# Where a convolution's filter spectra are computed: in three row norms, or tile by tile beside their use

## The chip, the cores and the metric

The kernel runs on one core of a Trainium2 chip. A core has a matrix engine (TensorE, PE in the profile), a vector engine (VectorE, DVE), a scalar engine (ScalarE, ACT), GpSimd (POOL) and the queue of SyncE (SP), which issues the transfers. They run side by side and wait for each other through semaphores. The metric is the device time of one execution in microseconds (us). Three executions of the kernel before took 2008.16, 2002.99 and 2000.46 us, median 2002.99 us.

## The reference, cut to what matters

256 tokens of width 1024 go through two transformer layers (attention and a gated feed-forward part each), then through a block that mixes a gated recurrence (HGRN) with a long convolution (Hyena), and through a large expert layer. What the change touches is the convolution's filter, one per channel:

```python
    h_f, h_b = hyena_filters(L, filt_w1, filt_b1, filt_freq1, filt_w2, filt_b2, filt_freq2,
                             filt_w3, filt_decay)
    y_b = x0 * bidirectional_fftconv(v * x1, h_f, h_b, hyena_bias)
...
    uf = jnp.fft.rfft(uf32, n=2 * L, axis=1)
    kf = jnp.fft.rfft(kern, n=2 * L, axis=0)
    y = jnp.fft.irfft(uf * kf[None], n=2 * L, axis=1)[:, :L]
```

`kern` is put together from the forward and the backward taps, which come from weights alone. So `kf`, the filter's spectrum, does not depend on the tokens and can be computed at any time before the product. The kernel computes both spectra by multiplying with a table of cosines and sines (`dft`, for a transform of length 511): the real part of the filter's from the sum of the two taps (`filt_sum`), the imaginary part from their difference (`filt_dif`).

## The kernel before, in words

Everything is held with channels on the 128 partitions and the 256 tokens beside each other, so a matrix of width 1024 is eight column tiles. Weights come in slabs of 128 x 1024 through a ring of three buffers. ScalarE copies each slab to a rounded "lead" (L260), VectorE subtracts to get the "rest" (L266), and TensorE multiplies both parts (L282, L401, L414). The order of the work on each engine is written out by hand; no scheduler moves anything.

**The row norms.** There are four stages "p0" to "p3", one after each half of the two layers. In each, ScalarE squares a half of the rows (L642), takes the root (L645), VectorE the reciprocal (L697), both scale it (L648, L699), and TensorE turns it back with eight transposes (L684), once for each half of the tokens. Then VectorE adds to the residual `xT` (L704), ScalarE and VectorE make the parts `hsplit` for the next stage (L726, L736), and TensorE begins with it (L401, 12 matmuls for each quarter of the channels). After p0, p1 and p2 there is also a late norm (L749, 32 records of one column) after the third quarter.

**The spectra.** `spectrum_tensor` (L658) computes the spectrum of one channel tile with four matmuls of 256 columns in full float32 (L664), each of which is two records in the profile. The tiles are spread as `SPECTRA_AT` says: none in p0, three in p1, three in p2, two in p3, the first behind the first eight transposes and the others behind the second eight. ScalarE copies them later to `filt_sum` and `filt_dif` (L671), over the taps that they were made from, so nothing else is held. `spectra_read_tensor` makes TensorE wait for the copies before it uses the banks again.

**Clearing the feed-forward output.** Each feed-forward stage clears four PSUM banks with four matmuls of zeros (L462). In layer 0 that stands behind the row norm p0. In layer 1 the spectra lie in these banks, so it stands after the fourth quarter.

**The Hyena stage.** It runs once for each of the eight channel tiles n. On TensorE (`hyena_tile_tensor`): transposes of the input u (L2193), one slab of weights for the next tile (24 matmuls, "filler", L282), the spectrum of u (L2198), two more fillers, transposes of the product (L2206), a fourth filler, and the inverse transform (L2211). On VectorE (`hyena_tile_vector`): the rest of a slab, a part of the HGRN norm (L2158 to L2160), the two spectral products (L2298), the sum and difference (L2303, L2304), rests of slabs and the short convolution that makes the next u. On ScalarE: the copies of the PSUM results and the leads. At n = 0 there is also one root over 2048 columns (L2153) of the sums in banks 4 to 7.

Of the kernel before, what the change touches and what calls it, by code (L numbers as in the profile page):

```python
# [30 lines left out]
P = 128  # L31
D = 1024
# [94 lines left out]
def build(nc, weights, small, tables, masks, w3, decay, subkeys, gain_row, x, out):  # L127
# [309 lines left out]
    def ffn_tensor(pe, layer, pre):  # L437
# [35 lines left out]
        if layer == 1:  # L473
            clear()
# [25 lines left out]
    def ffn_scalar(act, layer, pre):  # L500
# [27 lines left out]
        if layer == 1:  # L528
            spectra_scalar(act, "p2")
# [122 lines left out]
    SPECTRA_AT = {"p0": (), "p1": (0, 1, 2), "p2": (3, 4, 5), "p3": (6, 7)}  # L652

    def spectrum(n):

        return strided(filt_sum, n * P, [[2 * D, 2], [D, 2], [1, P]])

    def spectrum_tensor(pe, st, k):  # L658
        n = SPECTRA_AT[st][k]
        if n == 0:  # L660
            pe.wait_ge(S("filters", "taps"), FILTER_BLOCKS - 2)
        for part, taps in enumerate((filt_sum, filt_dif)):
            for a in range(2):
                mm = pe.matmul(ps[:, 1 + k, part * T:(part + 1) * T], taps[:, a, n * P:(n + 1) * P],  # L664
                               dft[:, a, part * T:(part + 1) * T], start=(a == 0), stop=(a == 1))
        mm.then_inc(S("hyena", "spectra"), 1)

    def spectra_scalar(act, st):
        for k, n in enumerate(SPECTRA_AT[st]):
            act.wait_ge(S("hyena", "spectra"), n + 1)  # L670
            act.activation(spectrum(n), ps[:, 1 + k, :].rearrange("p (b a c) -> p b a c", b=2, a=2),  # L671
                           ACT.Copy).then_inc(S("hyena", "spectra_sb"), 1)

    def spectra_read_tensor(pe, st):
        pe.wait_ge(S("hyena", "spectra_sb"), SPECTRA_AT[st][-1] + 1)

    def rows_norm_tensor(pe, st):
        for tt in range(TT):
            for c in range(KC):
                if c == 0:  # L680
                    pe.wait_ge(S("rows", "scalar"), rows_at(st, 6, 3 * tt + 3))
                if c == 4:
                    pe.wait_ge(S("rows", "vector"), rows_at(st, 4, 2 * tt + 2))
                mm = pe.transpose(YB[:, c, tt * P:(tt + 1) * P], y_rows[:, tt, c * P:(c + 1) * P], eye)  # L684
                if tt == TT - 1 and c % 2:
                    mm.then_inc(S("rows", "tensor"), 1)
            for n in range(len(SPECTRA_AT[st])):
                if min(n, 1) == tt:
                    spectrum_tensor(pe, st, n)
# [112 lines left out]
    dft = table("dft").rearrange("p (a f) -> p a f", a=2)  # L802
# [182 lines left out]
    def fox_scalar(act, st):  # L985
# [32 lines left out]
        act.wait_ge(S("hgrn", "bounds"), 1)  # L1018
        act.activation(lbe, lbd, ACT.Exp).then_inc(S("hgrn", "bounds"), 1)
# [109 lines left out]
    def moba_tensor(pe, st):  # L1129
        pe.wait_ge(S("norm", "x"), x_steps("p1") + 2)  # L1130
        for g, bank in enumerate((4, 2)):
            if g == 1:
                spectra_read_tensor(pe, "p1")
            for q in range(4):
# [3 lines left out]
                if g == 1 and q == 1:  # L1138
# [3 lines left out]
                    mm.then_inc(S(st, "factor"), 1)  # L1142
# [58 lines left out]
    def moba_scalar(act, st):  # L1201
# [12 lines left out]
        spectra_scalar(act, "p1")  # L1214
# [35 lines left out]
    def moba_vector(v, own, st):  # L1250
# [33 lines left out]
        v.wait_ge(S(st, "factor"), 2)  # L1284
# [622 lines left out]
    def hgrn_tensor(pe, st):  # L1907
# [8 lines left out]
        for j in range(5):  # L1916
            if j == 2:
                spectra_read_tensor(pe, "p3")
# [89 lines left out]
    def hgrn_scalar(act, st):  # L2008
# [13 lines left out]
        spectra_scalar(act, "p3")  # L2022
# [77 lines left out]
    def bounds_logits_vector(v, own, st):  # L2100
        l2 = small_("lbl").rearrange("p (a h) -> p a h", a=2)
        own(v.tensor_tensor(lbs, l2[:, 0, :], l2[:, 1, :], ALU.max))
        v.tensor_tensor(lbd, l2, lbs.unsqueeze(1).to_broadcast([P, 2, HH]), ALU.subtract).then_inc(S(st, "bounds"), 1)

    def bounds_vector(v, own, st):
        v.wait_ge(S(st, "bounds"), 2)
# [62 lines left out]
    uT = carve(TT, P)  # L2169
    prod_a, prod_b = carve(2, T), carve(2, T)  # L2170
    yspec = carve(4, P)
    yspecT = carve(4, P)
    conv_y = carve(T)
    idft = table("idft").rearrange("p (a f) -> p a f", a=4)
# [15 lines left out]
    def hyena_tile_tensor(pe, st, n):  # L2190
# [39 lines left out]
    def hyena_tile_scalar(act, st, n):  # L2230
# [5 lines left out]
        lead_scalar(act, *filler(4 * n + 2))  # L2236
        lead_scalar(act, *filler(4 * n + 3))
# [49 lines left out]
    def hyena_tile_vector(v, own, st, n):  # L2287
# [4 lines left out]
        if n == 0:  # L2292
            v.wait_ge(S(st, "spectra_sb"), KC)
        v.wait_ge(S(st, "uspec"), n + 1)

        def times(dst, part):
            half = ps[:, 3, part * T:(part + 1) * T].rearrange("p (a c) -> p a c", a=2)
            return v.tensor_tensor(dst[:, :, :].rearrange("p b (a c) -> p b a c", a=2),  # L2298
                                   half.unsqueeze(1).to_broadcast([P, 2, 2, P]), spectrum(n), ALU.mult)
        times(prod_a, 0)  # L2300
        own(times(prod_b, 1))
        f = yspec[:, :, :].rearrange("p a c -> p (a c)")
        v.tensor_tensor(f[:, 0:T], prod_a[:, 0, :], prod_b[:, 1, :], ALU.subtract)  # L2303
        v.tensor_tensor(f[:, T:2 * T], prod_a[:, 1, :], prod_b[:, 0, :], ALU.add).then_inc(S(st, "yspec"), 1)  # L2304
# [251 lines left out]
    def early_tensor(pe, st, stream):  # L2556
        pe.wait_ge(S("final", "x_rows"), 2)
# [31 lines left out]
    def picks_vector(v, own, st):  # L2589
# [15 lines left out]
        v.wait_ge(S("final", "x_rows"), 2)  # L2605
# [181 lines left out]
    def x_rows_tensor(pe, pre):  # L2787
# [4 lines left out]
        mm.then_inc(S("final", "x_rows"), 1)  # L2792

    def x_rows_scalar(act):
        act.wait_ge(S("final", "x_rows"), 1)
# [384 lines left out]
```

## Time and profile before

| | |
|---|---|
| Three executions | 2008.16, 2002.99, 2000.46 us |
| The profiled execution | 2008.16 us, of which the traced span is 2006.1 us |
| TensorE busy (matmul records) | 1954.2 us, 97% |
| TensorE weight loads busy | 1728.1 us, 86% |
| VectorE busy | 1340.2 us, 67% |
| ScalarE busy | 1008.5 us, 50% |
| Mean granted TensorE clock | 0.983 of full |

The profiled execution is the slowest of the three. TensorE's matmul records overlap, so its share is an upper view of its work. PEclk in a row is the share of the full clock that was granted in that stretch: 1.00 is 2.4 GHz and 0.50 is 1.2 GHz.

### The profile page before, as it was taken

To read this page: it belongs to the slowest core of one execution; us is meant where nothing else is said; L and a number is where in the kernel's file an instruction comes from. 1 tells how busy PE (TensorE), PEld (TensorE's weight loads), DVE (VectorE), ACT (ScalarE), POOL (GpSimd) and SP (SyncE) were. 2 spreads that over 40 slices of the span, in tenths; PEclk is the share of its full clock that TensorE was granted. 3 is DMA by queue.
4 is the path that set the end of the run, shared out by engine and by line. 5 is a ranking of instruction groups with operands and counts; after the bars stand their busy time and mean duration, and the time that the engine had idled before them with its cause. 6 is when DMAs were issued, how large, how long until landed. Compare 5 with 4: busy or idle time off the path is not lost.

```text
span 2006.1 us, 34432 instructions
## 1 busy us (share of the span) xinstructions
PE 1954.2 (97%) x12338; PEld 1728.1 (86%) x12338; DVE 1340.2 (67%) x2732; ACT 1008.5 (50%) x1632; POOL 320.4 (16%) x138
## 2 busy tenths in 40 slices
PE   7998999999999999999999999999999999999998
PEld 6775788778788888999899989999999998888886
DVE  6356556656655557889898689933667766666666
ACT  5336546555554446666544455665444443433333
POOL 0000000000000000000000057877666600000000
PEclk9799899999999999999999999999999999999999
DMA  6142465544335554444344535555444455555554
GB/s 230 62 150 73 147 209 180 162 132 137 102 130 189 188 188 137 148 144 131 105 143 143 178 126 169 181 174 168 138 140 145 137 162 195 190 197 188 195 191 157
DMA packets 85150, 313.99 MB, mean 157 GB/s; under 512 B 9456, under 2 KB 9456, under 8 KB 84592
## 3 DMA queue, kind: packets, MB, share of 16 engines
q1 hardware_dynamic: 85040, 312.49, 47.2%
q8 instruction: 73, 1.20, 0.3%
q14 instruction: 37, 0.30, 0.1%
HBM read 311.40 MB, written 1.05 MB: 156 GB/s over the span
## 4 chain that ended last, share of the span: by engine, by line
issue 61%; PE 32%; POOL 6%; DVE 0%; POOLq 0%; DVEq 0%; ACT 0%
PE ps L414 17%; PE ps L282 12%; POOL wsplit L266 6%; PE ps L2683 3%; PE ps L430 0%; DVE work L2813 0%; DVE sq L2720 0%; POOLq L265 0%; PE ps L2759 0%; POOLq L2546 0%; DVE sq L2716 0%; DVE picks L2636 0%; PE ps L2649 0%; DVEq L2971 0%; DVE work L2728 0%
## 5 line engine op out<-in xcount | busy, mean ns | idle before, releaser
L260 ACT ACTIVATE wsplit<-ring 128x1024 fp32r<-128x1024 f32 x572 | 603.8, 1057 | 506.4 <-PE ps L414 268.9
L266 DVE TENSOR_TENSOR wsplit<-ring,wsplit 128x1024 fp32r<-128x1024 f32 x438 | 535.0, 1224 | 330.0 <-ACT wsplit L260 328.5
L282 PE MATMUL ps<-hsplit,wsplit 128*128 128x256 f32 x5064 | 652.3, 288 | 7.1 <-DVE hsplit L736 2.1
L282 PEld LDWEIGHTS ps<-hsplit,wsplit 128*128 128x128 f32 x5064 | 625.3, 194 | 18.0 <-issue 9.1
L266 POOL TENSOR_TENSOR wsplit<-ring,wsplit 128x1024 fp32r<-128x1024 f32 x134 | 320.2, 2396 | 1291.3 <-ACT wsplit L260 1291.3
L414 PE MATMUL ps<-wsplit,gsplit 128*128 128x512 f32 x1992 | 456.5, 390 | 0.0
L414 PEld LDWEIGHTS ps<-wsplit,gsplit 128*128 128x128 f32 x1992 | 373.2, 188 | 81.5 <-issue 4.2
L401 PE MATMUL ps<-wsplit,hsplit 128*128 128x512 f32 x1248 | 305.7, 402 | 12.6 <-DVE wsplit L266 10.7
L401 PEld LDWEIGHTS ps<-wsplit,hsplit 128*128 128x128 f32 x1248 | 238.2, 193 | 64.9 <-issue 13.8
L1825 PE MATMUL ps<-hsplit,wsplit 128*128 128x256 f32 x936 | 128.5, 288 | 0.0
L1825 PEld LDWEIGHTS ps<-hsplit,wsplit 128*128 128x128 f32 x936 | 116.3, 191 | 0.0
L2720 DVE TENSOR_SCALAR sq<-ps,picks 128x128 f32<-128x128 f32 x256 | 87.0, 404 | 0.0
L2740 DVE TENSOR_TENSOR work<-ps,work 128x216 f32<-128x216 f32 (+31 forms) x64 | 32.9, 514 | 74.0 <-ACT work L2708 74.0
L2382 PE MATMUL ps<-hsplit,wsplit 128*128 128x256 f32 x576 | 71.4, 285 | 0.7 <-DVE hsplit L2363 0.4
L2382 PEld LDWEIGHTS ps<-hsplit,wsplit 128*128 128x128 f32 x576 | 69.7, 192 | 2.1 <-DVE wsplit L266 0.8
L2683 PE MATMUL ps<-sq 128*128 128x128 f32 x512 | 67.6, 275 | 0.3 <-DVE sq L2720 0.3
L2696 ACT ACTIVATE work<-ps 128x252 f32<-128x252 f32 (+62 forms) x63 | 17.5, 278 | 99.7 <-PE ps L282 99.7
L2683 PEld LDWEIGHTS ps<-sq 128*128 128x128 f32 x512 | 62.6, 192 | 0.5 <-DVE sq L2720 0.5
L1936 ACT ACTIVATE work<-work 128x256 f32<-128x256 f32 x128 | 48.7, 430 | 23.8 <-DVE work L2078 17.8
L304 DVE TENSOR_TENSOR gsplit<-work,gsplit 128x256 fp32r<-128x256 f32 x128 | 54.4, 425 | 4.4
L2567 ACT ACTIVATE work<-ps 128x256 f32 x54 | 20.8, 385 | 58.2 <-PE ps L282 58.1
L1894 PE MATMUL ps<-work 128*128 128x128 f32 x288 | 43.9, 275 | 0.7 <-ACT work L1936 0.7
(316 smaller groups left out, 1697.7 us busy)
## 6 DMA issues: line engine op xcount, KB each, us to landing
ring<-in_weights SPq DMA_DIRECT2D x580, 512.0 KB, 3.3
work<-in_tables SPq DMA_DIRECT2D x1, 2123.0 KB, 12.6
xT<-in_x SPq DMA_DIRECT2D x1, 1024.0 KB, 5.1
work<-in_subkeys SPq DMA_DIRECT2D x1, 1024.0 KB, 15.2
work<-in_decay SPq DMA_DIRECT2D x2, 512.0 KB, 4.1
out_x<-work SPq DMA_DIRECT2D x2, 512.0 KB, 2.6
work<-in_w SPq DMA_DIRECT2D x1, 512.0 KB, 6.6
ring<-in_gain_row SPq DMA_DIRECT2D x1, 512.0 KB, 3.7
```

What stands on the lines that cost most here:

```text
L260: act.activation(wsplit[:, n % RING, 0, :], slab(s), ACT.Copy).then_inc(S("split", "lead"), 1)
L266: eng.tensor_tensor(wsplit[:, n % RING, 1, :], slab(s), wsplit[:, n % RING, 0, :], ALU.subtract).then_inc(S("split", RESTS[stream][0]), 1)
L282: mm = pe.matmul(dst, wsplit[:, n, a, c * P:(c + 1) * P], hsplit[:, b, c, :], start=(c == 0 and t == 0), stop=(c == KC - 1 and t == 2))
L304: v.tensor_tensor(gsplit[:, slot, 1, :], src, gsplit[:, slot, 0, :], ALU.subtract).then_inc(sem, 1)
L401: mm = pe.matmul(ps[:, bank + tt, :], hsplit[:, b, c, tt * P:(tt + 1) * P], wsplit[:, n, a, cc * 512:(cc + 1) * 512], start=(c == 0 and t ...
L414: mm = pe.matmul(YR[:, tt, half * 512:(half + 1) * 512], gsplit[:, slot, b, tt * P:(tt + 1) * P], wsplit[:, n, a, half * 512:(half + 1) * ...
L1825: mm = pe.matmul(dst, wsplit[:, n, a, c * P:(c + 1) * P], hsplit[:, b, c, :], start=(c == 0 and t == 0), stop=(c == KC - 1 and t == 2))
L1894: mm = pe.matmul(dst[:, a, :], k_[:, a * P:(a + 1) * P], q_[:, b * P:(b + 1) * P], start=True, stop=True)
L1936: ins = act.activation(strided(mixed, (l % 2 * 2 + x_) * T, [[2 * size, n], [size, 2], [1, size]]), strided(qakb, x_ * 2 * T, [[2 * size, ...
L2382: mm = pe.matmul(branch(m), wsplit[:, n, a, c * P:(c + 1) * P], hsplit[:, b, c, :], start=(c == 0 and t == 0), stop=(c == KC - 1 and t == 2))
L2683: mm = pe.matmul(ps[:, 6 + b % 2, k * P:(k + 1) * P], hots[:, b % 2, 1, k, :], hots[:, b % 2, 0, k, :], start=True, stop=True)
L2720: ins = v.tensor_scalar(hots[:, b % 2, 0, k, :], ps_iota, picks[:, 0, t:t + 1], picks[:, 2, t:t + 1], ALU.is_equal, ALU.mult)
```

## The change

The spectra are no longer computed in the row norms. Each is computed in the Hyena stage, in its own tile, between the spectrum of u and the second filler, in PSUM bank 4. ScalarE copies it to a new buffer `kspec` with two activations (512 columns, and 256 columns of the cosine part again), and the VectorE product waits for these. The products are the same in number and shape, only their operands are laid out otherwise. The clear of layer 1 stands where that of layer 0 stands. At n = 0 the wait for the root of the HGRN norm moves ahead of the new matmuls, since that root reads bank 4. Some semaphores are split into two names, which changes no order.

```diff
-        def clear():
-            if layer == 1:
-                spectra_read_tensor(pe, "p2")
-            for y in range(4):
-                pe.matmul(ps[:, y, :], zeros[:, :], zero_rows(), start=True, stop=False, skip_group_check=True)
-
-        if layer == 0:
-            clear()
+        for y in range(4):
+            pe.matmul(ps[:, y, :], zeros[:, :], zero_rows(), start=True, stop=False, skip_group_check=True)
         pe.wait_ge(S("norm", "x"), x_steps(POST[pre]) + 2)
...
         pe.wait_ge(S("late", "scalar"), LATE_NORMS.index(pre) * 5 + 5)
-        if layer == 1:
-            clear()
...
-    SPECTRA_AT = {"p0": (), "p1": (0, 1, 2), "p2": (3, 4, 5), "p3": (6, 7)}
...
-            for n in range(len(SPECTRA_AT[st])):
-                if min(n, 1) == tt:
-                    spectrum_tensor(pe, st, n)
...
     # hyena_tile_tensor
         for a in range(TT):
-            mm = pe.matmul(ps[:, 3, :], uT[:, a, :], dft[:, a, :], start=(a == 0), stop=(a == 1))
-        mm.then_inc(S(st, "uspec"), 1)
+            pe.matmul(ps[:, 3, :], uT[:, a, :], dft[:, a, :], start=(a == 0), stop=(a == 1))
+        if n == 0:
+            pe.wait_ge(S("hnorm", "root"), 1)
+        for part, taps in enumerate((filt_sum, filt_dif)):
+            for a in range(2):
+                mm = pe.matmul(ps[:, 4, part * T:(part + 1) * T], taps[:, a, n * P:(n + 1) * P], dft[:, a, part * T:(part + 1) * T],
+                               start=(a == 0), stop=(a == 1))
+        mm.then_inc(S(st, "spectra"), 1)
         filler_tensor(pe, st, n, 1)
         filler_tensor(pe, st, n, 2)
-        if n == 0:
-            pe.wait_ge(S("hnorm", "root"), 1)
         pe.wait_ge(S(st, "yspec"), n + 1)
...
     # hyena_tile_scalar
         lead_scalar(act, *filler(4 * n + 2))
+        act.wait_ge(S(st, "spectra"), n + 1)
+        act.activation(kspec[:, 0:2, :].rearrange("p a t -> p (a t)"), ps[:, 4, :], ACT.Copy).then_inc(S(st, "kspec"), 1)
+        act.activation(kspec[:, 2, :], ps[:, 4, 0:T], ACT.Copy).then_inc(S(st, "kspec"), 1)
         lead_scalar(act, *filler(4 * n + 3))
...
     # hyena_tile_vector
-        if n == 0:
-            v.wait_ge(S(st, "spectra_sb"), KC)
-        v.wait_ge(S(st, "uspec"), n + 1)
...
+        v.wait_ge(S(st, "kspec"), 2 * n + 1)
+        uspec = ps[:, 3, :].rearrange("p (a t) -> p a t", a=2)
+        v.tensor_tensor(prod_a[:, :, :], uspec, kspec[:, 0:2, :], ALU.mult)
+        v.wait_ge(S(st, "kspec"), 2 * n + 2)
+        own(v.tensor_tensor(prod_b[:, :, :], uspec, kspec[:, 1:3, :], ALU.mult))
```

On TensorE, in the feed-forward stage of layer 1, this stood in a row before, from the end of the attention output (L788) over the row norm p2 to the first quarter inside the loop:

```order
L788 MATMUL ps<-wsplit,hsplit 128x512 x24
L684 MATMUL ps<-eyeiota,work 128x128 x8
L664 MATMUL ps<-work 128x256 x4
L684 MATMUL ps<-eyeiota,work 128x128 x8
L664 MATMUL ps<-work 128x256 x8
L401 MATMUL ps<-wsplit,hsplit 128x512 x36
L749 MATMUL ps<-ones,sq 128x1 x16
L401 MATMUL ps<-wsplit,hsplit 128x512 x12
L462 MATMUL ps<-zeros 128x512 x4
```

The same place in the changed kernel (its lines 750, 649, 459 and 711 are 788, 684, 462 and 749 before):

```order
L750 MATMUL ps<-wsplit,hsplit 128x512 x24
L649 MATMUL ps<-eyeiota,work 128x128 x16
L459 MATMUL ps<-zeros 128x512 x4
L401 MATMUL ps<-wsplit,hsplit 128x512 x36
L711 MATMUL ps<-ones,sq 128x1 x16
L401 MATMUL ps<-wsplit,hsplit 128x512 x12
```

Twelve float32 matmuls are gone between and behind the transposes, and the four clears have moved ahead of the quarters. In p1 and p3 the spectra go too (12 and 8 matmuls), and nothing takes their place.

One tile of the Hyena stage on TensorE before, from the transposes of u to the inverse transform:

```order
L2193 MATMUL ps<-eyeiota,work 128x128 x2
L282 MATMUL ps<-hsplit,wsplit 128x256 x24
L2198 MATMUL ps<-work 128x512 x2
L282 MATMUL ps<-hsplit,wsplit 128x256 x48
L2206 MATMUL ps<-eyeiota,work 128x128 x4
L282 MATMUL ps<-hsplit,wsplit 128x256 x24
L2211 MATMUL ps<-work 128x256 x4
```

The same tile in the changed kernel, where L2160 is the spectrum of the filter:

```order
L2150 MATMUL ps<-eyeiota,work 128x128 x2
L282 MATMUL ps<-hsplit,wsplit 128x256 x24
L2155 MATMUL ps<-work 128x512 x2
L2160 MATMUL ps<-work 128x256 x4
L282 MATMUL ps<-hsplit,wsplit 128x256 x48
L2167 MATMUL ps<-eyeiota,work 128x128 x4
L282 MATMUL ps<-hsplit,wsplit 128x256 x24
L2172 MATMUL ps<-work 128x256 x4
```

Four matmuls of 256 columns are added to each of eight tiles; the rest stands as it stood.

## Rows read from the trace of the kernel before

**Rows 1.** The page's busy times: engine, us, share of the span, instructions.
```profile
PE 1954.2 (97%) x12338; PEld 1728.1 (86%) x12338; DVE 1340.2 (67%) x2732; ACT 1008.5 (50%) x1632; POOL 320.4 (16%) x138
```

**Rows 2.** Timeline, Hyena tile 0: start, us, engine, line, operation, count, idle before.
```profile
970.81 1.97 ACT L2153 ACTIVATE work<-ps,eps_tile 128x2048 f32<-128x2048 f32 x1
...
973.10 6.30 PE L282 MATMUL ps<-hsplit,wsplit 128*128 128x256 f32 x48
...
977.85 1.28 DVE L2298 TENSOR_TENSOR work<-ps,work 128x512 f32<-128x512 f32 x2
...
980.08 0.63 PE L2206 MATMUL ps<-eyeiota,work 128*128 128x128 f32 x4 [0.67 <-DVE work L2304]
981.12 3.13 PE L282 MATMUL ps<-hsplit,wsplit 128*128 128x256 f32 x24 [0.41 <-DVE wsplit L266]
...
987.20 3.13 PE L282 MATMUL ps<-hsplit,wsplit 128*128 128x256 f32 x24 [1.01 <-DVE wsplit L266]
```

**Rows 3.** Windows, one later Hyena tile: PE, PEld, DVE, ACT, POOL busy, clock, DMA.
```profile
1018.60:1034.20 15.60, 15.60 (x117) 14.39 (x116) 14.94 (x25) 6.25 (x9) 0.00 (x0) 1.00 0.40 136
```

**Rows 4.** Timeline of that tile, the steps that the new matmuls touch.
```profile
1021.33 1.88 PE L2198 MATMUL ps<-work 128*128 128x512 f32 x4
...
1024.13 1.28 DVE L2298 TENSOR_TENSOR work<-ps,work 128x512 f32<-128x512 f32 x2
...
1032.10 1.89 PE L2211 MATMUL ps<-work 128*128 128x256 f32 x8
1032.20 2.36 DVE L266 TENSOR_TENSOR wsplit<-ring,wsplit 128x1024 fp32r<-128x1024 f32 x2
...
1033.83 0.38 PE L2193 MATMUL ps<-eyeiota,work 128*128 128x128 f32 x2
```

**Rows 5.** Line 671, the copy of a spectrum: count, ns min/median/max, first and last start.
```profile
L671 ACT ACTIVATE work<-ps x8: 575/584/600, 439.7 to 786.9; 128x512 f32<-128x512 f32 x8
```

**Rows 6.** Timeline of TensorE, row norm p0 and the start behind it (no spectra).
```profile
216.94 1.09 PE L684 MATMUL ps<-eyeiota,work 128*128 128x128 f32 x8 [1.58 <-ACT work L648]
...
220.30 10.99 PE L401 MATMUL ps<-wsplit,hsplit 128*128 128x512 f32 x36 [1.30 <-DVE hsplit L736]
231.13 3.63 PE L749 MATMUL ps<-ones,sq 128*128 128x1 f32 x32
...
241.80 0.60 PE L446 MATMUL ps<-eyeiota,sq 128*128 128x128 f32 x4
```

**Rows 7.** The same for row norm p1 (three spectra).
```profile
427.18 1.09 PE L684 MATMUL ps<-eyeiota,work 128*128 128x128 f32 x8
428.11 3.62 PE L664 MATMUL ps<-work 128*128 128x256 f32 x16
431.38 8.74 PE L401 MATMUL ps<-wsplit,hsplit 128*128 128x512 f32 x36
439.95 3.62 PE L749 MATMUL ps<-ones,sq 128*128 128x1 f32 x32
```

**Rows 8.** The same for row norm p2 (three spectra, clear in the later place).
```profile
567.30 1.09 PE L684 MATMUL ps<-eyeiota,work 128*128 128x128 f32 x8
...
588.06 1.03 PE L462 MATMUL ps<-zeros 1*128 1x512 bf16 x4
589.03 3.06 PE L401 MATMUL ps<-wsplit,hsplit 128*128 128x512 f32 x12
591.92 0.60 PE L446 MATMUL ps<-eyeiota,sq 128*128 128x128 f32 x4
```

**Rows 9.** The same for row norm p3 (two spectra, norm of the HGRN input).
```profile
765.88 1.09 PE L684 MATMUL ps<-eyeiota,work 128*128 128x128 f32 x8
...
769.24 2.99 PE L401 MATMUL ps<-wsplit,hsplit 128*128 128x512 f32 x12 [0.54 <-DVE hsplit L736]
772.07 3.61 PE L365 MATMUL ps<-sq,ones 128*128 128x256 f32 x16
```

**Rows 10.** Windows behind p0, p1 and p3, columns as in rows 3.
```profile
218.00:220.00 2.00, 1.00 (x5) 0.26 (x4) 1.81 (x5) 1.67 (x4) 0.00 (x0) 0.73 0.00 0
224.00:226.00 2.00, 2.00 (x7) 1.57 (x6) 1.75 (x5) 2.00 (x5) 0.00 (x0) 0.57 0.09 35
...
430.00:432.00 2.00, 2.00 (x10) 1.74 (x10) 2.00 (x4) 0.27 (x1) 0.00 (x0) 1.00 0.00 0
...
769.00:770.00 1.00, 0.76 (x3) 0.67 (x4) 1.00 (x2) 1.00 (x3) 0.00 (x0) 1.00 0.00 0
```

More of the change, by code:

```diff
@@ L650, in rows_norm_scalar @@
             lead_scalar(act, leads, 1)
-    SPECTRA_AT = {"p0": (), "p1": (0, 1, 2), "p2": (3, 4, 5), "p3": (6, 7)}
[L654 to L659, printed above, removed]
-        if n == 0:
[L661 to L675, printed above, removed]
     def rows_norm_tensor(pe, st):
@@ L801, in build @@
     SEGS = ((1, 0, T), (0, T, P))
-    dft = table("dft").rearrange("p (a f) -> p a f", a=2)
     pos[0] = era
@@ L1017, in fox_scalar @@
         act.preload_act_table(ACT.Exp)
-        act.wait_ge(S("hgrn", "bounds"), 1)
-        act.activation(lbe, lbd, ACT.Exp).then_inc(S("hgrn", "bounds"), 1)
+        act.wait_ge(S("hgrn", "lbd"), 1)
+        act.activation(lbe, lbd, ACT.Exp).then_inc(S("hgrn", "lbe"), 1)
         lead_scalar(act, st, 6)
@@ L1283, in moba_vector @@
         moba_rest(v, 6)
-        v.wait_ge(S(st, "factor"), 2)
+        v.wait_ge(S(st, "factors"), 1)
         by_token = ps[:, 7, 0:T].unsqueeze(1).to_broadcast([P, 2, T])
@@ L2102, in bounds_logits_vector @@
         own(v.tensor_tensor(lbs, l2[:, 0, :], l2[:, 1, :], ALU.max))
-        v.tensor_tensor(lbd, l2, lbs.unsqueeze(1).to_broadcast([P, 2, HH]), ALU.subtract).then_inc(S(st, "bounds"), 1)
+        v.tensor_tensor(lbd, l2, lbs.unsqueeze(1).to_broadcast([P, 2, HH]), ALU.subtract).then_inc(S(st, "lbd"), 1)
     def bounds_vector(v, own, st):
-        v.wait_ge(S(st, "bounds"), 2)
+        v.wait_ge(S(st, "lbe"), 1)
         own(v.tensor_tensor(lbs, lbe[:, 0, :], lbe[:, 1, :], ALU.add))
@@ L2169, in build @@
     uT = carve(TT, P)
+    kspec = carve(3, T)
     prod_a, prod_b = carve(2, T), carve(2, T)
@@ L2173, in build @@
     conv_y = carve(T)
+    dft = table("dft").rearrange("p (a f) -> p a f", a=2)
     idft = table("idft").rearrange("p (a f) -> p a f", a=4)
@@ L2291, in hyena_tile_vector @@
             hgrn_norm_vector(v, own, "hnorm", n)
-        if n == 0:
-            v.wait_ge(S(st, "spectra_sb"), KC)
-        v.wait_ge(S(st, "uspec"), n + 1)
[L2296 to L2301, printed above, removed]
+        v.wait_ge(S(st, "kspec"), 2 * n + 1)
[3 more added lines that the diff above has]
+        own(v.tensor_tensor(prod_b[:, :, :], uspec, kspec[:, 1:3, :], ALU.mult))
         f = yspec[:, :, :].rearrange("p a c -> p (a c)")
-        v.tensor_tensor(f[:, 0:T], prod_a[:, 0, :], prod_b[:, 1, :], ALU.subtract)
-        v.tensor_tensor(f[:, T:2 * T], prod_a[:, 1, :], prod_b[:, 0, :], ALU.add).then_inc(S(st, "yspec"), 1)
+        v.tensor_tensor(f[:, 0:T], prod_a[:, 0, :], prod_a[:, 1, :], ALU.subtract)
+        v.tensor_tensor(f[:, T:2 * T], prod_b[:, 0, :], prod_b[:, 1, :], ALU.add).then_inc(S(st, "yspec"), 1)
         rest_of(v, *filler(4 * n + 3))
@@ L2556, in early_tensor @@
     def early_tensor(pe, st, stream):
-        pe.wait_ge(S("final", "x_rows"), 2)
+        pe.wait_ge(S("final", "x_rows"), 1)
         with pe.Fori(0, EARLY // 6) as i:
@@ L2603, in picks_vector @@
             own(v.tensor_scalar(best[:, tt, 0:6, :], best[:, tt, 0:6, :], row_stats[:, 2, tt:tt + 1], None, ALU.mult))
-        v.wait_ge(S("final", "x_rows"), 2)
+        v.wait_ge(S("final", "x_rows"), 1)
         v.tensor_copy(ps_iota, iota)
@@ L2791, in x_rows_tensor @@
                 mm = pe.transpose(YR[:, tt, c * P:(c + 1) * P], xT[:, c, tt * P:(tt + 1) * P], eye)
-        mm.then_inc(S("final", "x_rows"), 1)
+        mm.then_inc(S("final", "x_turned"), 1)
     def x_rows_scalar(act):
-        act.wait_ge(S("final", "x_rows"), 1)
+        act.wait_ge(S("final", "x_turned"), 1)
         act.activation(x_rows[:, :, :], YR, ACT.Copy).then_inc(S("final", "x_rows"), 1)
```

10 lines of the change are left out of this document (1 added, 9 removed).

## The prediction

> **What bounds the kernel now.** I read the page first. TensorE's matmul records fill 97% of the span [rows 1], but they overlap, so this alone does not say that a microsecond more of matmul is a microsecond more of time. That has to be read at the two places of the change: where the spectra leave, and where they go.
>
> Where they go is the Hyena stage. The windows of one tile [rows 3] show TensorE busy for all of 15.60 us, VectorE 14.94 and ScalarE 6.25, with the clock at 1.00. The timeline of TensorE repeats with 15.58 us from tile to tile and has no idle entry from tile 1 to tile 6, and one of a few tenths at most at tile 7. So in tiles 1 to 7 TensorE is the bound, with VectorE close behind. Tile 0 is different [rows 2]: there TensorE waits 0.67 us for VectorE's product (L2304), 0.41 us for a slab's rest and 1.01 us for the next one (L266). VectorE sets that tile.
>
> Where they leave is the row norms. p0 has no spectra and the feed-forward stage behind it is built like the one behind p2. So p0 is a model, in this very trace, of what p2 becomes, and nearly one for p1. [Rows 6] show that TensorE idles 1.58 us ahead of the second transposes and 1.30 us ahead of the first quarter, and [rows 10] that the granted clock is 0.73 over 218 to 220 us and 0.57 over 224 to 226 us, and 0.50 between: it is at its lower level, 1.2 GHz, from about 218.9 to 225.7 us. Ahead of that fall TensorE had done nothing but transposes, waits and the four clears since 214.3 us. Behind p1 and p3 the clock reads 1.00 [rows 10]; there the spectra stood between and behind the transposes.
>
> **The Hyena stage.** The added work is four float32 matmuls of 256 columns for each tile, two records each. The trace has the same form in the inverse transform L2211: 8 records from 1032.10 us, and the next operation starts at 1033.83 [rows 4], so 1.73 us. The two spectra in a row in p1 agree: 16 records in 3.62 us, the tail of the last included [rows 7]. In tiles 1 to 7 there is no idle time to hide this: 7 x 1.73 = 12.1 us.
>
> In tile 0 the new matmuls would begin where the second filler begins, at 973.10 us. The root that they now wait for ends at 970.81 + 1.97 = 972.78 [rows 2], so that wait costs nothing, by 0.3 us. The 1.73 us push the product's transposes from 980.08 to about 981.1, since the 0.67 us of waiting goes. Then the slab's rest comes on time (0.41 goes), and the third wait, 1.01 us for a rest that VectorE delivers at 987.2 by its own chain, takes up what is left of 1.73 - 0.67 - 0.41 = 0.65 us. So tile 0 costs 0, if VectorE is not delayed there. If it is by the whole amount, 1.7 us; I keep that end for the range.
>
> Is VectorE delayed? The changed product waits for ScalarE's copy of the spectrum. In a tile the product starts 2.80 us after the spectrum of u begins (1021.33 to 1024.13 [rows 4]). After the change the matmuls end at about 1.3 + 1.73 = 3.05 us, the first copy takes 0.58 us [rows 5] with some 0.3 us of waking, so the product starts at about 3.95, 1.1 us later. The second copy has half the columns, so at most 0.58 us, and ends while the first product (0.64 us) runs. VectorE's 14.94 us and this 1.1 us are 16.0, under the new tile of 15.6 + 1.7 = 17.3. Queued behind the waiting product are the sum and difference, the slab's rest, the short convolution and the next u. What TensorE needs of these latest is the next slab's rest: VectorE starts it at 1032.20, has it at about 1033.4, and TensorE wants it at about 1034.0 [rows 4]. It moves by 1.1 us and TensorE by 1.7, so the slack grows. In tile 0 VectorE reaches its product only at 977.85 us [rows 2], long after the copies (about 976.0), so nothing is added. ScalarE has 6.25 of 15.6 us busy [rows 3]; 1.2 us more, between two leads, fits. Its lead for the fourth filler comes some 2 us later, still ahead of VectorE's rest of it.
>
> The Trainium skill would price these matmuls otherwise. "TensorE: Matmul & The Clock Gate", section "Back-to-back issue gap", lists 262 cycles for 256 columns, 0.11 us at full clock. By that table an added tile would be 4 x 0.11 = 0.44 us and seven of them 3.1 us, and the whole change about +7 us. The row on the same form shows two records a matmul and 1.73 us for four, so the trace does not agree with that figure for float32 operands, and the measurement decides.
>
> The Trainium skill's front page, "Trainium Kernel Development and Optimization", section "Best Practices", also says to judge TensorE by the share of weight loads and not by matmul busy time. That share is 14.39 of 15.60 us in a tile [rows 3], which read so would leave 1.2 us per tile for the new work and make the seven tiles 7 x 0.5 = 3.7 us. I do not take it, because the added work is itself a stream of load and matmul pairs behind a stream of the same.
>
> **The row norms.** p2: from the second transposes to the first transposes of the loop (L446) it is 591.92 - 567.30 = 24.62 us before [rows 8], and 241.80 - 216.94 = 24.86 us in p0 [rows 6]. That is the changed order exactly, clears included, so +0.24 us. It is made of two parts that nearly cancel: the quarters start earlier and the clears leave the busy stretch (588.06 to 589.03, 1.0 us), but the three quarters run partly at 1.2 GHz (10.99 against 8.74 us, [rows 6, 7]).
>
> p1: from the second transposes to the late norm it is 439.95 - 427.18 = 12.77 us [rows 7], and 231.13 - 216.94 = 14.19 us in p0 [rows 6]: +1.42 us. There the quarters would begin 3.36 us after the transposes in place of 4.20 (a gain of 0.84), and lose 2.25 to the clock. p1 has no clear to move.
>
> p3: TensorE started its first quarter 3.36 us after the transposes already [rows 9], as in p0, and it waited 0.54 us, so nothing is gained. The loss is that of p0, 2.25 us, if the clock falls. Part lies on the first 12 matmuls (2.99 us at full clock) and the rest on the sums L365 behind them, and the root, the reciprocal and the whole norm of the HGRN input hang on these sums. So I take +2.2 us, all on the path. Bounds for p1 and p3: with no fall -0.84 and 0; with all of the first stretch at the lower level the 8.74 us of [rows 7] would double, so +7.9 and, by the 6.6 us of [rows 9], +6.6. The nearest row is p0, and I use it.
>
> ScalarE's eight copies (0.58 us each) leave these stages; no wait of TensorE hangs on them, so 0.
>
> **The sum.** 12.1 + 0 + 0.24 + 1.42 + 2.2 = 16.0 us. The profiled execution took 2008.16 us with a span of 2006.1, so its counterpart would have a span of 2022.1 and take 2024.2. The median of before lies 5.2 us under the profiled one, so as a median I forecast 2003.0 + 16.0 = 2019.0 us.
>
> **The rivals.**
>
> *The clock does not fall.* Transposes and short gaps do not bring it down in p1, p2 and p3. For it: in p3 before, TensorE idled about half a microsecond at 1.00. Against it: p0. Then the norms give -0.84, -0.84 - 1.0 and 0, together -2.7, and the change is +9.4: 2012.4 us, at the edge of 0.5%. If only one of p1 and p3 keeps its clock, it is about 2.2 less than forecast, 2016.8.
>
> *VectorE becomes the bound of the Hyena tiles.* The product waits for ScalarE, and something behind it, the next u or a rest, comes too late for TensorE. For it: 14.94 of 15.60 us busy [rows 3]. Against it: the slack worked out above. If each of seven tiles lost the whole 1.1 us again: +7.7, so 2026.7 us.
>
> *VectorE is the bound of these tiles already.* This is the one that ends without a loss that can be told. If TensorE's full busy time in tiles 1 to 7 hid slack, as its 2.1 us in tile 0 did, the matmuls would vanish in it and only the norms would be left: 2003.0 + 3.9 = 2006.9 us. It decides so only if VectorE's own chain needs 17.3 us for a tile; its busy time is 14.94, and TensorE has no wait entry there, which is why it is small.
>
> **How the numbers follow.** Forecast 0.78; the clock does not fall (anywhere) 0.08; VectorE late behind the copies 0.07; VectorE the bound already 0.04; the rest 0.03, of which 0.01 for a kernel that gains. 0.5% is 10 us, about what a measurement of this kernel can tell from no change, so the line is at 2013.0. Slower by over 0.5%: 0.78 + 0.07 + about a quarter of 0.08 + 0.01 = 0.88. Within: 0.11. Faster: 0.01. The range: the low end is the case without a fall of the clock, 2012.4; the high end takes 1.7 for tile 0 and some 3 us more of low clock, 2024, and 2 us more for the scatter of medians in executions that spread over 7.7 us. So 2012 to 2026.
>
> **What would show it.** Hyena tiles 1 to 6 at 17.3 us each in place of 15.58, TensorE without idle entries. Tile 0 as long as before, its 0.67 and 0.41 us gone and about 0.35 us of the third wait left. A product that starts about 1.1 us later in its tile. The clock near 0.5 for some 5 us behind p1, p2 and p3. From p1's second transposes to its late norm 14.2 us, and 24.9 us for p2's stretch. The forecast is wrong if the tiles grow by clearly less than 1.7 us, or if the clock behind p1 and p3 reads 1.00.

## The result, and the profile after

The changed kernel took 2016.21 us in the median of four executions (2012.11 to 2020.97), the kernel before 2001.72 us (four, 1998.60 to 2008.16). The ratio is 1.0076, 95% interval 1.0057 to 1.0094: 15 us slower, 11 to 19. The forecast was a loss of 16.0 us.

The two traces by themselves say less: the span is 2011.9 us against 2006.1, 5.8 us more. The difference from the 14.5 us between the medians lies in work that the change does not touch, and this is the first thing to read. The second transposes of p0 stand at 216.94 us before [rows 6] and at 210.08 after, with nothing changed ahead of them but the lines' numbers and two semaphores' names. Here are two windows of that part in the trace of the kernel before (columns as in [rows 3]):

```profile
50.00:60.00 10.00, 9.25 (x52) 8.59 (x52) 4.59 (x15) 4.41 (x12) 0.00 (x0) 0.75 0.15 53
90.00:100.00 10.00, 9.10 (x43) 7.68 (x43) 3.52 (x14) 3.92 (x11) 0.00 (x0) 0.53 0.11 35
```

And the same two windows in the trace of the changed kernel:

```profile
50.00:60.00 10.00, 9.25 (x57) 7.11 (x57) 3.82 (x8) 3.41 (x12) 0.00 (x0) 1.00 0.34 109
90.00:100.00 10.00, 10.00 (x81) 10.00 (x81) 4.91 (x9) 6.04 (x8) 0.00 (x0) 0.94 0.32 107
```

The granted clock reads 0.75 and 0.53 in the one and 1.00 and 0.94 in the other: it fell at other moments of the same sequence. So I compare the traces stage by stage, between operations that both have, and not by their ends. From the start to the second transposes of p0 the changed kernel's trace is 6.9 us shorter, from there to p1's 1.0 and on to p2's 2.1 us shorter. From p2's to p3's it is equal to 0.1 us. Then it is 1.6 us longer up to the Hyena stage, 11.9 us longer in it and 2.3 us longer behind it: 5.8 us in all. Of the last 2.3 us, 1.6 are one more spell at the lower clock (0.50 from 1654.5 to 1657.9 us), which the traces of two experiments on the kernel before have as well.

**Hyena.** TensorE's timeline of tiles 0 and 1 in the changed kernel (start, us, engine, line, operation, count, idle before):

```profile
960.30 0.38 PE L2150 MATMUL ps<-eyeiota,work 128*128 128x128 f32 x2
...
965.11 1.89 PE L2160 MATMUL ps<-work 128*128 128x256 f32 x8
966.65 6.10 PE L282 MATMUL ps<-hsplit,wsplit 128*128 128x256 f32 x48
972.59 0.60 PE L2167 MATMUL ps<-eyeiota,work 128*128 128x128 f32 x4
972.94 3.12 PE L282 MATMUL ps<-hsplit,wsplit 128*128 128x256 f32 x24
...
978.79 3.14 PE L282 MATMUL ps<-hsplit,wsplit 128*128 128x256 f32 x24 [0.79 <-DVE wsplit L266]
```

In tile 0 the waits of 0.67 and 0.41 us [rows 2] are gone and the third has shrunk from 1.01 to 0.79 us. From the first transposes to the next tile's first filler it is 978.79 - 960.30 = 18.49 us; before, 987.20 [rows 2] - 968.69 = 18.51, counted from this row of the kernel before:

```profile
968.69 0.38 PE L2193 MATMUL ps<-eyeiota,work 128*128 128x128 f32 x2
```

The waits were worth more than their entries say. The product's transposes start 12.29 us behind the first ones where it was 11.39, so 0.90 of the 1.73 us came through and the wait of 0.67 had been worth 0.83. The filler behind them starts 0.35 us later where it was 1.04, so the wait of 0.41 had been worth 0.69. An idle entry counts from the end of the last record, and without a wait the next operation starts before that end (the four transposes' row lasts 0.60 us, and the filler starts 0.35 us into it). The later tiles follow each other in 17.31 us where it was 15.58. One window of 17.30 us, which answers to [rows 3]:

```profile
1030.00:1047.30 17.30, 17.30 (x124) 15.88 (x123) 14.97 (x25) 7.01 (x11) 0.00 (x0) 1.00 0.38 122
```

TensorE is busy for all of it, VectorE for 14.97 us (14.94 before). The steps of tile 1, which answer to [rows 4]:

```profile
999.08 1.88 PE L2155 MATMUL ps<-work 128*128 128x512 f32 x4
...
1000.80 1.89 PE L2160 MATMUL ps<-work 128*128 128x256 f32 x8
...
1002.72 0.60 ACT L2199 ACTIVATE work<-ps 128x512 f32<-128x512 f32 x1 [4.98 <-PE ps L2160]
1003.22 0.38 ACT L2200 ACTIVATE work<-ps 128x256 f32<-128x256 f32 x1
...
1003.35 0.69 DVE L2258 TENSOR_TENSOR work<-ps,work 128x512 f32<-128x512 f32 x1 [1.40 <-ACT work L2199]
```

The product starts 4.27 us behind the spectrum of u (it was 2.80), 1.47 us later and not 1.1. The spectrum's records begin 1.72 us behind those of u, where I had 1.3, and the filler behind them starts at 1002.34, so the stream is through after 3.26 us and not 3.05. From there to the copy are 0.38 us, where I had 0.3.

**The row norms.** TensorE behind the second transposes of p1, p2 and p3, answering to [rows 7 to 9]:

```profile
419.31 1.09 PE L649 MATMUL ps<-eyeiota,work 128*128 128x128 f32 x8 [1.58 <-ACT work L638]
422.67 9.80 PE L401 MATMUL ps<-wsplit,hsplit 128*128 128x512 f32 x36 [2.26 <-DVE hsplit L698]
432.31 3.63 PE L711 MATMUL ps<-ones,sq 128*128 128x1 f32 x32
...
557.38 1.09 PE L649 MATMUL ps<-eyeiota,work 128*128 128x128 f32 x8 [1.57 <-ACT work L638]
560.74 10.71 PE L401 MATMUL ps<-wsplit,hsplit 128*128 128x512 f32 x36 [0.77 <-DVE hsplit L698]
...
581.95 0.60 PE L446 MATMUL ps<-eyeiota,sq 128*128 128x128 f32 x4
...
755.91 1.09 PE L649 MATMUL ps<-eyeiota,work 128*128 128x128 f32 x8 [1.58 <-ACT work L638]
759.27 4.58 PE L401 MATMUL ps<-wsplit,hsplit 128*128 128x512 f32 x12 [2.27 <-DVE hsplit L698]
763.68 3.62 PE L365 MATMUL ps<-sq,ones 128*128 128x256 f32 x16
```

Three windows of the same trace, behind the second transposes of p1, p2 and p3:

```profile
424.00:426.00 2.00, 2.00 (x7) 1.54 (x6) 2.00 (x7) 0.91 (x2) 0.00 (x0) 0.59 0.59 174
559.00:565.00 6.00, 5.23 (x13) 3.49 (x12) 5.68 (x13) 3.27 (x9) 0.00 (x0) 0.50 0.26 87
760.00:762.00 2.00, 2.00 (x6) 1.53 (x5) 2.00 (x6) 0.97 (x4) 0.00 (x0) 0.54 0.28 47
```

Each first quarter now has an idle entry ahead of it. The clock falls behind all three norms: it is at 0.50 for 3.4 us behind p1 and behind p3 (the windows of 2 us lie mostly in these spells) and for 6.8 us behind p2, where the prediction had some 5 us at each. p1's stretch is 13.00 us (12.77 before), p2's 24.57 (24.62), p3's to the sums 7.77 (6.19).

### The profile page after: what moved, and what is told of

Read it like the earlier page. It is cut to its first block, busy times and chain, and to the rows that moved or that the text cites. A ratio compares the mean times of both kernels' runs of the same rounds, so it can differ in the third digit from the quotient of the medians.

```text
span 2011.9 us, 34435 instructions
## 1 busy us (share of the span) xinstructions
PE 1953.4 (97%) x12338; PEld 1727.1 (86%) x12338; DVE 1340.9 (67%) x2732; ACT 1010.4 (50%) x1640; POOL 320.4 (16%) x138
## 4 chain that ended last, share of the span: by engine, by line
issue 61%; PE 32%; POOL 6%; DVE 0%; POOLq 0%; DVEq 0%; ACT 0%
PE ps L414 17%; PE ps L282 12%; POOL wsplit L266 6%; PE ps L2642 3%; PE ps L430 0%; DVE work L2772 0%; DVE sq L2679 0%; POOLq L265 0%; PE ps L2718 0%; POOLq L2505 0%; DVE sq L2675 0%; DVE picks L2595 0%; PE ps L2608 0%; DVEq L2930 0%; DVE work L2687 0%
## 5 line engine op out<-in xcount | busy, mean ns | idle before, releaser
L401 PE MATMUL ps<-wsplit,hsplit 128*128 128x512 f32 x1248 | 310.0, 406 | 17.2 <-DVE wsplit L266 10.6
```

Source lines behind the costliest of these rows:

```text
L401: mm = pe.matmul(ps[:, bank + tt, :], hsplit[:, b, c, tt * P:(tt + 1) * P], wsplit[:, n, a, cc * 512:(cc + 1) * 512], start=(c == 0 and t ...
```

## The experiments

All but one are timed against the kernel before, on the same chip. "Stretch" is always from the second transposes to the late norm (p1), to the first transposes of the loop (p2), or to the sums (p3).

**Norms alone.** The changed kernel with the Hyena stage's spectra taken out, shown shortened. It leaves out the filter's spectrum and its copies, and the product takes the taps in its place, so what it computes is not the block:

```diff
     # hyena_tile_tensor, hyena_tile_scalar
-        for part, taps in enumerate((filt_sum, filt_dif)):
-            for a in range(2):
-                mm = pe.matmul(ps[:, 4, ...], taps[:, a, n * P:(n + 1) * P], dft[...], ...)
-        act.activation(kspec[:, 0:2, :]..., ps[:, 4, :], ACT.Copy)
-        act.activation(kspec[:, 2, :], ps[:, 4, 0:T], ACT.Copy)
     # hyena_tile_vector
-        v.tensor_tensor(prod_a[:, :, :], uspec, kspec[:, 0:2, :], ALU.mult)
+        v.tensor_tensor(prod_a[:, :, :], uspec, filt_sum[:, :, 0:T], ALU.mult)
...
```

> The changed kernel's row norms (no spectra in p1, p2, p3, early clear) with no spectrum of the filter in the Hyena stage either: the four matmuls and both copies of each tile are left out, and the products take the taps in place of spectra. Theory A (the spectra kept TensorE's clock up behind the norms, and their going costs there): Hyena tiles 1 to 6 at 15.6 us as in the kernel before; behind p1, p2 and p3 the clock at 0.5 for some 3 to 5 us; in all +2.5 to +4 us against before, of which p3 +1.6, p1 +0.2 to +1.4, p2 about 0. Theory B (the clock's falls are not caused by the change and the norms gain from the matmuls and the clear that leave): -2.7 us against before. Theory C (all of the change's time is in the norms): +14 us.

Ratio 1.0003 (0.9991 to 1.0015), so 0.6 us more, between 1.8 less and 3.0 more. Hyena tiles 15.58 us. Theory C is out. Theory B's 2.7 us less lies outside the interval, but so does my own sum of 3.9 us for the norms, and most of theory A's 2.5 to 4. The stretches say why. The clock did fall behind p1: its stretch is 14.35 us, and the row of its first three quarters takes 11.15 us in TensorE's timeline of this kernel, against 8.74 at full clock in [rows 7]:

```profile
420.03 1.09 PE L649 MATMUL ps<-eyeiota,work 128*128 128x128 f32 x8 [1.58 <-ACT work L638]
423.38 11.15 PE L401 MATMUL ps<-wsplit,hsplit 128*128 128x512 f32 x36 [2.26 <-DVE hsplit L698]
...
437.86 8.45 PE L401 MATMUL ps<-wsplit,hsplit 128*128 128x512 f32 x36
```

But my stretch of p1 ends at the late norm, and behind it the time comes back. The last row above is the next three quarters, at full clock. In the kernel before they stand behind the late norm with a spell at 1.2 GHz in them:

```profile
443.44 10.07 PE L401 MATMUL ps<-wsplit,hsplit 128*128 128x512 f32 x36
```

Up to the end of these quarters (L1100, before L1141) p1 takes 26.13 us here and 26.17 before. p2's stretch is 23.94, 0.7 us shorter, and from p3 to the Hyena stage it is 204.38 us in place of 202.81. Together 0.9 us, which agrees with the 0.6 us timed. So the eight spectra, some 14 us of matmul, cost next to nothing where they stood.

**The matmuls twice.** The kernel before, with four more matmuls in each tile that nobody reads:

```diff
         mm.then_inc(S(st, "uspec"), 1)
+        if n == 0:
+            pe.wait_ge(S("hnorm", "root"), 1)
+            pe.wait_ge(S(st, "spectra_sb"), KC)
+        for part, taps in enumerate((filt_sum, filt_dif)):
+            for a in range(2):
+                pe.matmul(ps[:, 4, part * T:(part + 1) * T], taps[:, a, n * P:(n + 1) * P], dft[...], ...)
...
-        if n == 0:
-            pe.wait_ge(S("hnorm", "root"), 1)
```

> The kernel before, all spectra in the norms as they were, and in each Hyena tile the four matmuls again, into bank 4, read by nobody; no copies, no new wait of VectorE. Theory A (the price of the Hyena stage is TensorE's own time): tiles 1 to 6 at 17.3 us, tile 0 no longer than before, +12 us in all. Rival (the price comes from the product waiting for ScalarE's copies): tiles stay at 15.6 us and the time within 2 us of before.

Ratio 1.0062 (1.0047 to 1.0076), 9 to 15 us more. TensorE's timeline of this kernel over one tile, from its inverse transform (L2216) to the filler in the next one:

```profile
1014.87 1.89 PE L2216 MATMUL ps<-work 128*128 128x256 f32 x8
...
1019.68 1.88 PE L2198 MATMUL ps<-work 128*128 128x512 f32 x4
1021.39 1.89 PE L2205 MATMUL ps<-work 128*128 128x256 f32 x8
1022.93 6.09 PE L282 MATMUL ps<-hsplit,wsplit 128*128 128x256 f32 x48
```

Tiles 2 to 6 take 17.31 us, tiles 0 and 1 together 35.70 as in the changed kernel (35.69), with no copy and no new wait on VectorE. With the experiment above it splits the change: the Hyena matmuls are the loss. The two ratios give 12.4 and 0.6 us, and the changed kernel measured 12.8 us on the same chip (below).

**Warm norms.** The changed kernel with matmuls that nobody reads put back where the spectra were:

```diff
+    WARM_AT = {"p0": 0, "p1": 3, "p2": 3, "p3": 2}
     # rows_norm_tensor, behind each half's transposes
+            for n in range(WARM_AT[st]):
+                if min(n, 1) == tt:
+                    warm_tensor(pe, st, n)    # four matmuls of 256 columns, float32
```

> The changed kernel with 3, 3 and 2 times four float32 matmuls put back at the places where the spectra stood in p1, p2 and p3, into banks that nobody reads; the spectra that count stay in the Hyena stage, and the clear stays early. Theory A (clock): the clock stays at 1.00 behind p1, p2 and p3 until the late norm; p1's stretch from the second transposes to the late norm 12.8 us, p3's first twelve matmuls 3.0 us in place of 4.6, and the time 2 to 4 us less than the changed kernel's, though work is added. Theory B (the matmuls in the norms cost their time, the clock is not theirs): 1.7 us more than the changed kernel, 0.84 in each of p1 and p2.

TensorE's timeline of this kernel behind the second transposes of p1:

```profile
423.29 1.09 PE L659 MATMUL ps<-eyeiota,work 128*128 128x128 f32 x8
424.22 3.62 PE L649 MATMUL ps<-work 128*128 128x256 f32 x16
427.49 8.73 PE L401 MATMUL ps<-wsplit,hsplit 128*128 128x512 f32 x36
```

p1's stretch is 12.77 us, p3's 6.18, and from p3 to the Hyena stage 202.76 us. The clock stays up where these matmuls stand: theory A on these two stretches. Whether matmuls of another kind would do the same was not tried. But p2 starts its quarter 5.45 us behind the transposes, since the matmuls and the early clear stand in a row there, and takes 24.40 us, no less than without them. Ratio 1.0059 (1.0041 to 1.0076) against 1.0064 for the changed kernel on the same chip: the 2 to 4 us forecast did not show. The ratios are 1 us apart and the medians 1.8, and neither can be told from nothing.

**The changed kernel again.**

> The changed kernel once more, for the ratio on this chip and for a second trace. Both theories: 1.0065 to 1.0085 against before. If the lower clock behind the norms belongs to the change, the stretches behind p1, p2 and p3 show it again, with lengths that differ by some tenths of a us to 1 us from the first trace; Hyena tiles 17.3 us to the hundredth.

Ratio 1.0064 (1.0050 to 1.0078), so 12.8 us, a little under the 1.0065 to 1.0085 expected; the interval overlaps the first. Tiles 17.30 and 17.31 us, p3 to the Hyena stage 204.30 (first trace 204.39). p1's stretch is 13.21 us and p2's 23.60, where the first trace had 13.00 and 24.57: one program, up to 1 us apart.

**Late copy.** The changed kernel with three more copies ahead of the one that the product waits for:

```diff
+        if n:
+            act.wait_ge(S(st, "kspec"), 2 * n)
+        for j in range(3):
+            act.activation(late_copy[:, j, :], ps[:, 4, :], ACT.Copy)
         act.activation(kspec[:, 0:2, :].rearrange("p a t -> p (a t)"), ps[:, 4, :], ACT.Copy).then_inc(S(st, "kspec"), 1)
```

> The changed kernel with three more copies of the same 512 columns on ScalarE ahead of the one that the product waits for, so the product starts 1.5 us later in each tile (0.5 us each). Theory A (VectorE's slack is what the next slab's rest has left before TensorE wants it, about 0.85 us in the changed kernel): from tile 1 on TensorE waits 0.6 to 0.8 us a tile for L266 ahead of the first filler, tiles at 17.9 to 18.1 us, and the kernel 4 to 6 us slower than the changed one. Rival (the slack is VectorE's idle time, 2.3 of 17.3 us): tiles stay at 17.3 us. Second rival (the late copy is passed on in full): 18.8 us a tile, +10 us.

In the timeline of this kernel, ScalarE's copies and VectorE's product in tile 2:

```profile
1007.53 1.58 ACT L2203 ACTIVATE work<-ps 128x512 f32<-128x512 f32 x3 [5.06 <-PE ps L2161]
1008.98 0.62 ACT L2204 ACTIVATE work<-ps 128x512 f32<-128x512 f32 x1
1009.63 0.69 DVE L2263 TENSOR_TENSOR work<-ps,work 128x512 f32<-128x512 f32 x1 [2.75 <-ACT work L2204]
```

And TensorE's, later in the same tile:

```profile
1019.00 3.14 PE L282 MATMUL ps<-hsplit,wsplit 128*128 128x256 f32 x24 [0.51 <-DVE wsplit L266]
```

VectorE's product waits 2.75 us (1.40 in the changed kernel) and starts 1.47 us later behind the spectrum of u. TensorE now has an entry of 0.51 us in each tile from tile 2 on, for the slab's rest that is queued behind the product on VectorE (the second fence, TensorE's row). The tiles take 18.08 us, 0.77 more, in the range of theory A, though its wait of 0.6 to 0.8 us reads 0.51; both rivals are out. Ratio 1.0084 (1.0067 to 1.0101), some 4 us over the changed kernel's, with intervals that overlap; the tiles are what shows it. So VectorE was near: of the 1.47 us, 0.77 came through, and a product about 0.7 us later would have begun to cost.

**One spectrum in tile 0.** The kernel before, with one of the eight moved:

```diff
-    SPECTRA_AT = {"p0": (), "p1": (0, 1, 2), "p2": (3, 4, 5), "p3": (6, 7)}
+    SPECTRA_AT = {"p0": (), "p1": (1, 2), "p2": (3, 4, 5), "p3": (6, 7)}
     # hyena_tile_tensor, at n == 0 behind the spectrum of u: the four matmuls, and one copy on ScalarE
```

> The kernel before with one spectrum moved, that of tile 0: out of p1, which then has two, and into Hyena tile 0 in the place that the changed kernel uses, with one copy. Theory A (tile 0 has waits that hide one spectrum, and p1's third spectrum holds up its first quarter): tiles 0 and 1 together 34.0 us as before, p1's first quarter 3.36 us behind the transposes in place of 4.20, its clock still 1.00, stretch to the late norm 11.9 to 12.0 us, in all about 0.8 us less than before, which the timing cannot tell from nothing. Rival (tile 0 hides nothing): tiles 0 and 1 together 35.7 us, and +0.9 us in all.

TensorE's timeline of this kernel in p1, from its first quarter on:

```profile
423.26 5.72 PE L401 MATMUL ps<-wsplit,hsplit 128*128 128x512 f32 x24 [0.54 <-DVE hsplit L736]
429.82 3.02 PE L401 MATMUL ps<-wsplit,hsplit 128*128 128x512 f32 x12 [0.84 <-DVE wsplit L266]
432.68 2.51 PE L749 MATMUL ps<-ones,sq 128*128 128x1 f32 x22
```

Tiles 0 and 1 together take 33.99 us (33.98 before): tile 0 hides a spectrum whole. p1's first quarter starts 3.35 us behind the transposes, 0.84 earlier, as expected. But its third quarter then waits 0.84 us for a slab's rest, and the stretch is 12.77 us as before. So p1's third spectrum cost nothing, and my 0.84 us of gain was never there. Ratio 1.0004 (0.9993 to 1.0016). In the same trace p2's stretch, in which nothing was changed, is 23.42 us where the kernel before has 24.6, since the clock does not fall behind its late norm.

**The kernel before again**, one execution, for its trace:

> The kernel before once more, for a second trace. If the lower clock at the end of the attention between p1 and p2 comes and goes from execution to execution, p1 to p2 is either 140.1 us (lower clock once) or 137.8 us; the stretches behind p1, p2 and p3 are the same as in the first trace within 0.1 us, and Hyena tiles 15.58 us.

p1 to p2 140.19 us, p1's stretch 12.77, p2's 24.63, p3's 6.16, tiles 15.58. But p0's stretch to its late norm is 13.23 us, where the first trace had the 14.19 on which the prediction built. The part p1 to p2 takes 140.1 to 140.7 us in five of the traces (both of before among them) and 137.8 to 138.1 in the six others, of which one (the last experiment) has matmuls added there. What stands in the norms does not sort them. What differs is one fall of the clock at the end of the attention, seen in a window of 4 us at the same place of the program. First the kernel before, as first profiled:

```profile
537.00:541.00 4.00, 3.26 (x12) 2.36 (x13) 2.10 (x6) 4.00 (x14) 0.00 (x0) 0.50 0.00 0
```

Then the changed kernel:

```profile
527.20:531.20 4.00, 2.85 (x24) 2.13 (x25) 3.00 (x15) 2.11 (x6) 0.00 (x0) 1.00 0.00 0
```

**Warm in p3 only.** As in the warm norms, with `WARM_AT = {"p0": 0, "p1": 0, "p2": 0, "p3": 2}`:

> The changed kernel with two times four float32 matmuls put back in p3 only, into banks that nobody reads. Theory A: the clock stays at 1.00 behind p3 and falls behind p1 and p2; first quarter to the sums 3.0 in place of 4.5 us, p3 to the Hyena stage 202.8 us in place of 204.3 to 204.4, so 1.6 us less than the changed kernel though 3.4 us of matmul are added. Rival: 204.3 us as in the changed kernel.

TensorE's timeline of this kernel in p3, the first quarter and the sums:

```profile
761.39 2.99 PE L401 MATMUL ps<-wsplit,hsplit 128*128 128x512 f32 x12 [0.53 <-DVE hsplit L711]
764.22 3.61 PE L365 MATMUL ps<-sq,ones 128*128 128x256 f32 x16
```

The first quarter takes 2.99 us in place of 4.58 and p3 to the Hyena stage 202.79 us in place of 204.3 to 204.4, with 3.4 us of matmul added. p1's stretch, without its matmuls, is 14.47. Theory A on the stage; the ratio of the whole, 1.0059 (1.0039 to 1.0078), cannot tell 1.6 us.

**Warm in more places.** The kernel before with unread matmuls in p0 and at the end of that attention:

```diff
+            if st == "p0":
+                warm(pe, 1, 4)
...
+            if last:
+                warm(pe, 0, 3)      # ahead of the last scores
...
+            if last:
+                warm(pe, 1, 2)      # ahead of the last values
```

> The kernel before with float32 matmuls that nobody reads put into waits of TensorE where the trace of before shows a fall of the clock: four behind each half's transposes in p0, three ahead of the last scores of the attention of layer 1 and two ahead of its last values. Theory A (work in the wait keeps the clock up and costs nothing): clock 1.00 behind p0 and at the end of that attention; p0's stretch to the late norm 12.8 us in place of 13.2 to 14.2, p1 to p2 137.8 to 138.4 us in every execution in place of either 137.9 or 140.2; in all 0 to 4 us faster than before, mean 2, which is at the edge of what the timing tells. Rival (the clock falls a little later instead, and the matmuls cost their own time): the same time or up to 2 us slower, and the lower clock shows again within some us of those places.

TensorE's timeline of this kernel in p2, the late norm and the last quarter:

```profile
569.64 4.48 PE L755 MATMUL ps<-ones,sq 128*128 128x1 f32 x32
573.98 5.33 PE L401 MATMUL ps<-wsplit,hsplit 128*128 128x512 f32 x12
```

p0's stretch is 12.79 us, shorter than in any other trace, and the fall behind its second transposes is gone, as theory A has it. p1 to p2 is 137.87 us, but five of the ten traces without these matmuls had that too, so one trace does not show it. Then p2's stretch is 26.24 us where it was 24.6: the late norm of one-column matmuls and the quarter behind it run at the lower clock for longer (4.48 and 5.33 us for 3.6 and 4.6). Ratio 0.9996 (0.9983 to 1.0010): nothing won that can be told. In this one trace 1.6 us of the gain went again in p2; whether that is so in every execution is open. No version measured beats the kernel before by more than its interval.

## Why the prediction was right, and where it was not

**The seven tiles: right.** 12.1 us forecast. From tile 0's first transposes to the end of the Hyena stage's last inverse transform it is 11.9 us more, 1.73 in each of tiles 1 to 6 and 1.5 in tile 7, and doubling the matmuls without any copy gives the same tiles. An added tile's matmuls cost 1.73 us and nothing of it went into the 1.2 us in which the weight loads are not busy. Neither estimate that the prediction worked out from the Trainium skill held here. The 0.44 us for a tile, an estimate from the Trainium skill's table in "TensorE: Matmul & The Clock Gate", section "Back-to-back issue gap", is a quarter of the 1.73 us measured. The Trainium skill's page "Trainium Kernel Development and Optimization", section "Best Practices", names MFU (the share of the peak rate of arithmetic) and the share of weight loads as measures of the distance to roofline. The room that the prediction read from the second, and did not take, was not there.

**Tile 0: right**, 0.0 us, shown twice (the changed kernel and the single moved spectrum). The way there was counted too dearly: I took the first two waits at their entries, 0.67 + 0.41, and left about 0.35 us of the third. They were worth 0.83 + 0.69, so only 0.21 us reached the third, which kept 0.79.

**VectorE beside it: right in kind, its wait too small.** The product came 1.47 us later and not 1.1, so VectorE's slack for the next slab's rest grew by 0.26 us a tile and not by 0.6. The slack was there, but the late copy shows that it was a slack of 0.7 to 0.8 us, and not the 2.3 us that busy times alone suggest. That is the reason to follow what is queued behind a wait instead of adding up busy shares.

**The norms: the step that was mis-sized.** I took 3.86 us (1.42, 0.24, 2.2). The norms alone measured 0.6 us, at most 3.0. For p1 I ended the stretch at the late norm, and that is the term that fails most: over the five traces with no spectra in p1 and p2 this stretch is 13.00, 14.35, 13.21, 13.25 and 14.47 us, a mean of 0.9 over before's 12.77, but up to the end of the next three quarters it is 26.38, 26.13, 26.55, 26.61 and 26.25, a mean of 0.2 over the 26.12 to 26.20 of the six others. Where the first spell was longest, the one behind the late norm was missing. p2's stretch is 24.57, 23.94, 23.60, 23.55 and 22.30, a mean of 1.0 under before's 24.6; but with the spectra in their old place it was itself 24.62, 24.63, 24.65, 23.42 and 26.24, so this difference lies inside the spread of one and the same code. p3 is the steady one: 204.30 to 204.39 against 202.76 to 202.82 us wherever matmuls stand there, 1.6 us. Together 0.8 us. Two things failed in my step. I used p0 of one trace as a constant, 14.19 us; the same unchanged code took 13.2 to 13.3 us in eight other traces and 14.27 in one. And I looked only at the first fall, and not at the second spell behind the late norm, which p1 and p2 had before the change too and which the earlier fall replaced in two traces each. The clock's fall itself, and that matmuls in the gaps prevent it, is shown by the warm norms and the p3 run.

**The sum.** 11.9 + 0.2 - 1.0 + 1.6 = 12.7 us. Another 0.7 us stands in the later query stage that GpSimd paces; TensorE shows it 254 us behind the Hyena stage's last inverse transform. It is in all four traces that have the changed kernel's Hyena stage as it is, and not in those of before, of the norms alone or of the late copy. I did not follow it; its cause stays open. 13.4 us is within both intervals of the changed kernel (11 to 19 and 10 to 16).

**The rivals.** "The clock does not fall" is refuted by the windows. "VectorE becomes the bound" did not happen, but the late copy shows where it would. "VectorE is the bound already" is refuted by tiles of 17.31 us. The forecast of the time, 2019.0 us, lies 2.8 us above the median. Of this, 1.3 us are the median of the kernel before, which the fourth execution moved, and 1.5 us the loss. The norms were too dear by some 3 us; that it shows so little is partly luck, as the 0.7 us above and the scatter between executions work the other way. The sum holds because three quarters of it are the tiles.

## What to carry to other kernels

Work that does not depend on the data was cheapest here in the waits of the engine that bounds the kernel: taking the eight spectra out of there saved nothing that can be told, and in each Hyena tile but the first one costs 1.73 us. Its price elsewhere is read from one window: where that engine has no idle entry, each microsecond added is a microsecond of time, even beside an engine at 96%. When matmuls leave a wait, ask also what kept the clock up there. End a stretch only where both kernels run alike again, since a fall that comes earlier can replace a later one. And for a difference under one per cent compare traces by stage, over several executions: here two traces differed by 6.9 us in a part that was the same in both.

## What the runs showed of the hardware

TensorE's clock falls at different moments of one and the same sequence. In the ten traces in which nothing was added there, the end of one attention ran at full clock in five and had a spell at 1.2 GHz in five, 2.3 us apart. Ahead of the first quarters of p1, p2 and p3, where TensorE had nothing but transposes, clears and waits for some 6 us, the quarters ran longer than at full clock in every trace without the spectra (p1's and p2's three took 9.76 to 11.29 us in place of 8.46 to 8.78), and in none with float32 matmuls between and behind the transposes. Such a spell made the stretches of p1 and p3 longer by 0.2 to 1.7 us. In p1 a second spell behind the late norm (three quarters in 9.8 to 10.1 us) stood in nine of the eleven traces; in the two others, where the first had lasted 6.8 us, these quarters ran at full clock in 8.45 us, and p1 up to their end was within 0.1 us of the kernel before.
